# Weighted expert sums of a PEER layer: gathers of 32 tokens x 4 slots, 32-column matmuls, a ring of 6 freed in pairs

## What is computed

```python
q = (xb @ w_pq).reshape(PEER_BLOCK, PEER_HEADS, 2, PEER_QDIM // 2)
s = jnp.einsum('phcd,hckd->phck', q, sub_keys).astype(jnp.float32)
ts, ti = lax.top_k(s, PEER_TOPK)
...
fs, fpos = lax.top_k(cand.reshape(PEER_BLOCK, PEER_HEADS, -1), PEER_TOPK)
eidx = jnp.take_along_axis(cidx.reshape(PEER_BLOCK, PEER_HEADS, -1), fpos, axis=-1)
g = jax.nn.softmax(fs, axis=-1)
u = u_tab[eidx]
v = v_tab[eidx]
a = jax.nn.gelu(jnp.einsum('pd,phkd->phk', xb, u).astype(jnp.float32), approximate=False)
return jnp.einsum('phk,phkd->pd', (g * a).astype(v.dtype), v)
```

## Time and profile before

| | |
|---|---|
| median of 3 runs | 2869.38 us (2855.88 to 2876.55) |
| span of the profiled execution | 2849.4 us; its own time is not recorded |
| busy: PE / DVE / ACT / POOL | 1959.6 / 1637.4 / 397.6 / 652.7 us |
| gathers and chunks, software DMA queue | 604.55 MB |

### The profile page before, as it was taken

How to read it: one execution, slowest core, us unless ns; L and a number is a source line. 1 busy time by engine, 2 the same in 40 slices (tenths; PEclk the granted TensorE clock), 3 DMA queues, 4 the chain that set the end, 5 groups by cost and what they waited for, 6 DMA issues and landing times.

```text
span 2849.4 us, 19084 instructions
## 1 busy us (share of the span) xinstructions
PE 1959.6 (69%) x6466; PEld 1073.8 (38%) x6466; DVE 1637.4 (57%) x3431; ACT 397.6 (14%) x993; POOL 652.7 (23%) x585
## 2 busy tenths in 40 slices
PE   7997789997786522677777776775666676852334
PEld 4433556695486411333233333332233232631110
DVE  3303733302369887565666666655765666477766
ACT  1101123211011100111111011101121111010010
POOL 0000000000000213343344343332433342232232
PEclk9998755556997766789889888997888887676677
DMA  3214160003000457899989999896988889885586
GB/s 109 89 74 34 5 212 1 1 1 158 34 1 1 173 207 321 363 382 363 372 345 357 378 373 360 329 372 261 365 345 317 339 330 403 351 354 236 236 332 266
DMA packets 114049, 680.20 MB, mean 239 GB/s; under 512 B 28768, under 2 KB 32544, under 8 KB 36448
## 3 DMA queue, kind: packets, MB, share of 16 engines
q0 software_dynamic: 83168, 604.55, 53.6%
q1 hardware_dynamic: 30784, 74.44, 8.1%
HBM read 672.55 MB, written 10.55 MB: 240 GB/s over the span
## 4 chain that ended last, share of the span: by engine, by line
PE 35%; DMA 21%; DVE 19%; POOL 7%; issue 5%; ACT 2%; POOLq 0%; DVEq 0%; ACTq 0%
PE bank L696 31%; DMA arena<-in_uv,arena 21%; POOL arena L677 7%; DVE arena L1635 4%; PE bank L708 3%; DVE arena L1430 3%; DVE arena L1427 2%; PE bank L1733 2%; DVE arena L1432 1%; ACT arena L1309 1%; DVE arena L1652 1%; DVE arena L1472 1%; DVE arena L1473 1%; DVE arena L1469 1%; ACT arena L1107 1%
## 5 line engine op out<-in xcount | busy, mean ns | idle before, releaser
L696 PE MATMUL bank<-arena 128*128 128x512 f32 (+13 forms) x4672 | 1513.1, 487 | 783.6 <-ACT arena L1309 658.4
L696 PEld LDWEIGHTS bank<-arena 128*128 128x128 f32 (+4 forms) x4672 | 809.4, 224 | 1423.3 <-ACT arena L1309 703.3
L677 POOL DMA_INDIRECT arena<-in_uv,arena x544 | 616.7, 1134 | 1671.2 <-PE bank L696 1537.7
L1635 DVE CUSTOM_DVE_ANT_0 arena<-arena 128x1024 f32<-128x1024 f32 x544 | 655.4, 1225 | 440.2 <-DMA arena<-in_uv,arena 436.5
L1652 DVE SCALAR_TENSOR_TENSOR arena<-arena 128x1024 f32<-128x1024 f32 x267 | 343.2, 1285 | 9.5
L1733 PE MATMUL bank<-arena 128*128 128x512 f32 (+13 forms) x972 | 312.0, 481 | 46.1 <-DVE arena L2086 15.3
L1733 PEld LDWEIGHTS bank<-arena 128*128 128x128 f32 (+3 forms) x972 | 157.9, 197 | 199.6 <-issue 160.9
L708 PE MATMUL bank<-arena 128*128 128x128 f32 (+3 forms) x716 | 141.5, 342 | 36.1 <-DVE arena L1395 11.8
L1304 ACT ACTIVATE arena<-arena 128x4 f32<-128x4 f32 x136 | 27.7, 204 | 881.6 <-DVE arena L1635 877.6
L1107 ACT ACTIVATE arena<-bank 128x512 f32<-128x512 f32 (+6 forms) x229 | 112.3, 517 | 231.4 <-PE bank L708 209.0
L708 PEld LDWEIGHTS bank<-arena 128*128 128x128 f32 (+3 forms) x716 | 97.2, 172 | 122.2 <-issue 73.5
(11 more groups left out here) (219 smaller groups left out, 683.4 us busy)
## 6 DMA issues: line engine op xcount, KB each, us to landing
arena<-in_w_pq SPq DMA_DIRECT2D x8, 2048.0 KB, 12.8
arena<-in_w_in SPq DMA_DIRECT2D x6, 2048.0 KB, 7.6
arena<-in_uv,arena POOLq DMA_INDIRECT x544, 11.0
arena<-in_w SPq DMA_DIRECT2D x4, 2048.0 KB, 13.8
arena<-in_w_out SPq DMA_DIRECT2D x4, 2048.0 KB
arena<-in_xT SPq DMA_DIRECT2D x1, 2176.0 KB, 8.5
arena<-in_C SPq DMA_DIRECT2D x1, 2064.0 KB, 10.3
out_s_C<-arena SPq DMA_DIRECT2D x1, 2064.0 KB
```

Source lines behind the costliest of these rows:

```text
L677: nc.gpsimd.indirect_dma_start(uv[r], None, i["uv"], bass.IndirectOffsetOnAxis(eidx_u[:, t, s0 + r:s0 + r + 1], 0))\
L696: return te.matmul(out, l, r, start=start, stop=stop)
L1635: last = ve.tensor_tensor_reduce(out=uv[r][:, 0:D], in0=uv[r][:, 0:D], in1=x_sb[:, t, :], scale=1.0, scalar=0.0, op0=ALU.mult, op1=ALU.add ...
```

## The change

A gather of a prompt tile now holds 32 tokens x 4 slots on its 128 partitions, as those of the samples did, and 4 gathers in turn cover the tile's four groups of 32 tokens. The weighted sum of every gather is a product of a 128 x 32 matrix (`pick4`: gate times Gelu, where partition and token agree) with v, accumulated in 32 partitions of banks 0 and 1. ACT makes it in two steps (`gate4` ahead, then `pick4`); `weigh_rows`, `w8`, `diag` and `acc_v` go. An iteration is a pair of 2 gathers. The ring has 6 buffers, and three pairs are in it; `s_free` frees a pair. As dots need x by 32 tokens on all 128 partitions, PE and ACT spread each tile's tokens into `XR` (4096 words on each partition) ahead of the tile, and the retrieval writes indices and gates in the new layout with 32 copies of 32 x 32. The table of weights is the same, and `AFTER` is computed for 256 iterations instead of 64.

```diff
-        NR = 8
+        NR = 6
+        NP = 2
...
-        IT0 = [sum(GATHERS[:t]) // NR for t in range(TILES)]
+        IT0 = [sum(GATHERS[:t]) // NP for t in range(TILES)]
...
             def iteration(j):
-                t, s0 = slots_of(j)
-                for r in range(NR):
-                    if j and r % 4 == 0:
-                        pool.wait_ge(s_free, 2 * (j - 1) + r // 4 + 1)
-                    if j and r % 4 == 2:
-                        pool.wait_ge(s_vf, 2 * (j - 1) + r // 4 + 1)
...
+                t, pair = pair_of(j)
+                if j >= NR // NP:
+                    pool.wait_ge(s_free, j - NR // NP + 1)
+                for g, k, grp, _ in pair:
+                    nc.gpsimd.indirect_dma_start(uv[g % NR], None, i["uv"],
...
+            def spread_tokens(t):
+                spread_at[t] = fills[0]
+                for grp in range(GJ):
+                    for c2 in range(2):
+                        r = slice(NS * grp, NS * grp + NS)
+                        fill(lambda bank: mm(bank[:, :], C("rep4")[r, :], x_sb[r, t, c2 * 512:c2 * 512 + 512]))
...
             def iteration(j):
-                for r in (0, 1, 4, 5):
...
-                        last = mm(PB[c2][0:M, :], diag[r][:, 0:M], uv[r][:, D + c2 * 512:D + c2 * 512 + 512],
...
+                pe_eng.wait_ge(s_dg, NP * (j + 1))
+                for c2 in range(2):
+                    for g, k, _, c in pair:
+                        n = k if t < PT else k // GJ
+                        last = mm(PB[c2][NS * c:NS * c + NS, :], pick4[g % NR],
+                                  uv[g % NR][:, D + c2 * 512:D + c2 * 512 + 512],
+                                  n == 0, k + (GJ if t == PT else 1) >= GS)
+                last.then_inc(s_free, 1)
...
+                act.wait_ge(s_dot, j + 1)
+                sc.activation(gel[:, g0:g0 + NP], dots[:, g0:g0 + NP], ACT.Gelu).then_inc(s_gl, 1)
+                act.wait_ge(s_gl, j + 1)
+                act.wait_ge(s_pk, NP * (j + 1))
...
+                for g, k, _, _ in pair:
+                    sc.activation(pick4[g % NR], gate4[g % NR], ACT.Copy, scale=gel[:, g % NR:g % NR + 1])\
+                      .then_inc(s_dg, 1)
...
-                link(ve.tensor_copy(eidx_u[0:R, t, :], fa[0:R, 0, :]))
+                for q in range(QB):
+                    for grp in range(GJ if t < PT else 1):
+                        ve.tensor_copy(eidx_u[NS * q:NS * q + NS, t, grp, :],
...
             for j in range(N_IT):
-                weigh_rows(j, 0)
-                dot_rows(j, 1)
-                weigh_rows(j, 1)
...
+                ends = j + 1 in IT0[1:]
+                if not ends:
+                    dot_rows(j + 1)
+                for _ in range(pieces_at(j)):
+                    next(todo)
```

More of the change, by code:

```diff
@@ L49 @@
 QB = P // NS
+GJ = P // NS
+GS = SLOTS // QB
 INW = 3360
@@ L368, in program @@
         ff = p5.take(256).rearrange("p (z s) -> p z s", z=2)
[L369 to L376, removed]
+        p6 = Place(work_end)
+        dots = p6.take(8)[:, 0:NR]
+        gel = p6.take(8)[:, 0:NR]
+        gate4 = [p6.take(NS) for _ in range(NR)]
+        pick4 = [p6.take(NS) for _ in range(NR)]
         uv = [p6.take(2 * D) for _ in range(NR)]
+        XR = p6.take(GJ * D).rearrange("p (j d) -> p j d", j=GJ)
         early = Place(CL["cos"][0], CW)
@@ L688, in rest_gpsimd @@
             pool.wait_ge(s_idx, TILES)
-            for j in range(N_IT, N_IT + GATHERS[PT] // NR):
+            for j in range(N_IT, N_ALL):
                 iteration(j)
@@ L1628, in pieces, with dot_rows @@
                 yield from retrieve(PT)
[L1630 to L1635, removed]
+            def dot_rows(j):
+                t, pair = pair_of(j)
+                for g, _, grp, _ in pair:
+                    if t < PT and j < IT0[t] + 2:
+                        dve.wait_ge(s_te, spread_at[t] + 2 * (grp + 1))
+                    dve.wait_ge(s_uv[g % NR], 16 * (g // NR + 1))
+                    last = ve.tensor_tensor_reduce(out=uv[g % NR][:, 0:D], in0=uv[g % NR][:, 0:D],
+                                                   in1=XR[:, grp, :] if t < PT else x_sb[:, PT, :],
@@ L1660, in rest_vector @@
+                settle(s_dot)
             dve.wait_ge(s_sf, 4 * PT)
             todo = pieces()
-            dot_rows(0, 0)
+            dot_rows(0)
             for j in range(N_IT):
-                weigh_rows(j, 0)
-                dot_rows(j, 1)
-                weigh_rows(j, 1)
-                if j + 1 in IT0[1:]:
+                ends = j + 1 in IT0[1:]
+                if not ends:
+                    dot_rows(j + 1)
+                for _ in range(pieces_at(j)):
+                    next(todo)
+                if ends:
@@ L1680, in rest_vector @@
-            dve.wait_ge(s_y, TILES)
-            layer_norm(2 * PT + 1, PT, 1, NS, PB).then_inc(s_fin, 1)
+            for j in range(N_IT + 1, N_ALL):
+                dot_rows(j)
+            dve.wait_ge(s_ysum, 1)
+            layer_norm(2 * PT + 1, PT, 1, NS, PB[2:4]).then_inc(s_fin, 1)
             settle(s_fin)
```

152 lines of the change are left out of this document (68 added, 84 removed).

## The result

The changed kernel takes 2945.01 us in the median of 4 runs (2934.84 to 2950.81), the kernel before 2864.41 (4 runs): the ratio is 1.0274, with a 95% interval of 1.0242 to 1.0307. It is slower by 80.6 us. The profiled execution took 2950.81 us, with a span of 2949.0, which is 99.6 us above the span of before. The prediction was 2906 us, slower, with a range of 2785 to 2985.

The account below looks back on a forecast made before the run. DMA engines' active time plus 294 us of rest was taken to bound the gather stage, only rest moving. Terms -13 + 14 + 45 - 34 - 2 + 27 = +37 us gave 2906 us, range 2785 to 2985.

Parts of the forecast that it names:

- Stops at chunks: Where POOL waits to issue a chunk with only one pair landing: rest of 5.8 us each in compression, 9.4 in attention.
- The clock term: At the 18 chunk stops PE idles and starts its piece at half clock: 1.5 us each, +27 us, bounds 0 and 54.
- Hidden runs: 32 runs of 16 hidden records on PE, 7.04 us against a 7.1 limit: 0 to 1.5 us each, 0.5 taken, 16 us.
- Retrieval of the samples: Fourth stretch: rest of 31 us (14, last piece 6, layer norm 8, clock 3) against 65 before, -34 us.
- First stretch: Up to the first compression chunks: DVE begins 8 us later; rest of 55 us against 68 before, -13 us.
- the five pieces: First five of a retrieval's six DVE pieces, 43 us in all: 9 us of rest plus 1 each at half clock, 14.
- the sixth piece: Last DVE piece of a retrieval (11 + 3 us) releases POOL, standing at the first chunk behind one pair: 18 us.
- Tile change: Layer norm at a tile's end: about 15 us from release to release against 11.9 in flight, rest 6 to 9, 8 taken.
- the compression term: Compression stretch: chunk stops 41, hidden runs 16 and two layer norms of 8, 73 us against 59 before, +14.
- Rival A: Chunk stops cost nothing more than today: 2773 us in full, chance 0.15; 2840 if half true, chance 0.18.
- Rival B: PE column groups don't overlap for rows of 512, a pair takes 3.7 us: +121, 3027 us, chance 0.08.
- Rival C: PE sits at half clock in the whole gather stage, lengthening runs of 16: +80, 2986 us, chance 0.12.

Follow-up runs that it names:

- late chunks: Changed kernel with each chunk issued behind the gathers of the third iteration after the piece it waits for, instead of the first: 2786.22 us, ratio 0.9731.
- the kernel before with late chunks: Kernel before the change with its chunks issued one iteration of 8 gathers later: 2865.76 us, ratio 0.9993.
- the complete kernel with both: Changed kernel, nothing left out, with a ring of 8, chunks at +3, each tile in two halves and spreading ahead of the pieces: 2603.05 us, ratio 0.9087.
- the run on the same columns: Changed kernel with both gathers of a pair accumulated in the same 32 columns, sums of the other groups left out: 3054.36 us, ratio 1.0663.
- contiguous slots: Changed kernel with chunks at +3 and slots dealt in blocks of 32, so the 32 small copies read contiguous columns: 2786.07 us, ratio 0.9701.

## Why the prediction was right, and by how much it was off

The direction and the mechanism held: one pair instead of 8 gathers stands between piece and chunk, POOL waits in order, and the DMA engines rest. The late chunks prove it by taking the loss away. The size was another matter: 1.3% was forecast and 2.7% came, at the upper edge of the forecast's own range of 2860 to 2950, and slower at all had only been given 0.50. By the prediction's own terms:

- **Stops at chunks.** Forecast: 5.8 us in compression and 9.4 in attention, plus 1.5 for the clock. The rest around each, summed from the trace, is 3.3 to 7.7 us at the 7 stops of compression, 42 in all, where 41 and 7 x 1.5 make 51. In attention it is 5.1 to 11.8 at 13 stops, 117 in all, where 75 + 20 + 10 and 11 x 1.5 make 121. So the stops were priced right, compression's 9 us too high. The clock term holds in part: in the 12 us before the chunk's issue the granted clock is 1.00 throughout at 4 of the 20 stops, three of them those of compression with the least rest (3.3 to 4.8 us), and at half for some of the time at the other 16. At half clock the pair takes 3.63 us instead of 1.91. The sign had been put as 6 to 10 us of rest after POOL's row of a chunk; most of it lies before that row, while POOL waits.
- **Hidden runs**: 0.5 us each, 16 in all, had been forecast. In the second and third stretch 19 runs of 16 hidden records have 0.5 to 3.6 us of rest right behind them, 40 us in all. Spread over all 32 runs that is 1.25 us each: inside the bounds of 0 to 1.5 that the prediction gave them, but well over the 0.5 taken. One of them, POOL's row behind a run whose weights are loaded from 1301.93 to 1308.46, and the DMA tenths from 1290 to 1330 us:

```profile
1311.60 1.63 POOL L685 DMA_INDIRECT arena<-in_uv,arena  x1 [7.08 <-PE bank L704]
```
```profile
DMA  9999999999999999999920037899999999999999
```

 With a ring of 8 and the chunks left where they were, one such rest (1.9 us) is left in compression.
- **Retrieval of the samples** and last stretch: -34 and -2 forecast, -36 and -7 measured. Which part of the change won it was not tested: POOL's waits for PE in the retrieval go from 133 us, 30.0 at the longest, to 91, 17.1 at the longest.
- **First stretch**: -13 forecast, +14 measured. This step failed, by 27 us. Gathers begin 14.3 us later and the first dot 22.6 us later (994.74 for 972.16), not 8. The copies:

```profile
986.72 3.07 DVE L1518 CAST arena<-arena 32x32 uint32<-32x32 f32 x16
...
991.63 3.07 DVE L1532 COPY arena<-arena 32x32 f32<-32x32 f32 x16
```

 32 copies take 6.1 us where one instruction took 0.23, so a retrieval is 5.9 us longer and three are 18. Each copy costs 0.19 us, not 0.08. The two rows are 0.08 apart, but what follows the second starts 0.18 later: that pair of rows shows the lower of two prices, and one such distance is no price. The other 5 us are no cost of the change: the first retrieval begins at 814.31 us in this execution and at 809.52 in that of before, but at 808.50 with late chunks, whose program is the same up to there, and at 813.39 in the kernel before with late chunks. Of the terms, the full ring was 28 us of rest (23 forecast), the five pieces 12 (14), the sixth piece with POOL's 24.1 us at the first chunk 19.5 (18). Two items had not been in the sum: 16 us (before 2) until the first gathers are under way, in a stretch that is counted from 949 us, and 7 of the first compression stop, which falls into it.
- **Tile change**: 8 us forecast. The rest around it is 19.5 us at the first and 16.3 at the second; against the two of 8 in the compression term this is 20 us more. At the last it is 7. The compression term, with the second tile change in it, came out at +56 (before 45 + 10, after 95 + 16), where +14 and 7 x 1.5 for the clock had been forecast. The 95 + 16 are 35 at the six stops that lie there, 36 at the two tile changes and 40 behind hidden runs. The DMA tenths from 1435 to 1475 us, PE's row ahead of it, the first drain of the spreading, the new tile's first pair, and POOL:

```profile
DMA  9999999999997200000000000000000078999999
```
```profile
1435.62 12.54 PE L704 MATMUL bank<-arena 128*32 128x512 f32 x28 [3.06 <-ACT arena L1335]
...
1447.41 0.60 ACT L1122 ACTIVATE arena<-bank 128x512 f32<-128x512 f32 x1 [11.84 <-PE bank L704]
...
1461.29 3.63 PE L704 MATMUL bank<-arena 128*32 128x512 f32 x8 [4.89 <-ACT arena L1335]
...
1465.19 1.57 POOL L685 DMA_INDIRECT arena<-in_uv,arena  x1 [23.70 <-PE bank L704]
```

 I had summed spreading, dots, statistics and the pair to 15 us from release to release. At POOL it was 26: the pair before had been issued just ahead of the 23.70 us of waiting. What I had not seen is a run of 8 hidden matmuls (16 records) behind the tile's last pair: the spreading stands behind it in PE's order, and only then come the drains, the dots, the statistics, two loads of ACT's function table (1.28 us each) and a pair at half clock. Without the spreading these two places rest 2.5 and 2.7 us, so it was the spreading and its place, and not the layer norm, that made the 8 too small. In the complete kernel with both, the spreading stands ahead of the piece.
- **Rival A** (the stops cost nothing more) fell with the rest around the stops, 178 us for 32, and with the late chunks. **Rival B** (no overlap of column groups) fell with the 1.91 us row and the run on the same columns, whose +109 lies near the 121 that had been worked out for it. **Rival C**: the clock of the long stretches is 0.86, 0.86, 0.80, not under 0.65.

By the windows the sum was 60 us short (37 for 97): 27 in the first stretch, 31 in compression with its tile changes and hidden runs, 9 in attention (+70 for 45 + 16), less 7 that the last two stretches gave beyond their terms. By the medians it was 44 short.

## What to carry to other kernels

Where an engine issues work in order and waits in the middle of it, count how much it has issued that is still to land when the thing that it waits for begins: that is the cover. The order sets it, and a deeper ring did not add to it here. When the unit of an iteration is made smaller (8 gathers to 2), every distance that was written as "one iteration later" shrinks with it; here the constant 1 should have become at least 3, and that alone was worth 159 us (4, which would put 8 gathers between again, was not run). Buffers traded away for a layout (8 to 6) have a price of their own: look for a loop order that needs less of the new layout at a time before giving up depth. And a term that was worked out to lie right at a limit (runs of 7.04 us against 7.1) should not be priced near its lower bound.

## What the runs showed of the hardware that was not expected

- Column groups of 32 overlap for fp32 rows of 512: 8 records in two groups take 1.91 us, in one group 3.62, at full clock. The drain at a change of tiling mode that the Trainium skill states (TensorEngine Tiling (Array Packing), Key Properties) is not to be seen in the rows: after a pair of 1.91 us that begins at 2061.48, the first 128-column record begins at 2063.32. No run isolates the switch, so its price stays open below what a row resolves; the 0.3 us that the prediction set for one stands in no row.
- Indirect gathers of 1 MB with 8 KB rows, back to back, kept the DMA engines at a share of 0.99 to 1.01 and 406 to 416 GB/s over 571 us.
- Copies of 32 x 32 on DVE, one behind the other, take 0.19 us each, strided or contiguous. The same 128 x 128 numbers took 0.23 us in one instruction and 3.07 in 16: what counted was the number of instructions.
- A ring of 8 instead of 6 buffers of 1 MB was worth 152 us (5%) although the DMA engines rested only 334 of 1923 us at a ring of 6. Two thirds of it is rest: in the compression stretch alone it went from 59 us (420 x 0.14) to 26 (378 x 0.07). The other third is a higher rate while active, 407 GB/s for 394.
- Between executions the same instructions began up to 6.5 us apart: the first retrieval at 808.50 us with late chunks and at 815.03 with contiguous slots. A shift of a few us in one profile is no cost until it is seen to stand in a row of its own.
